# A two-block network on one core: later heads' keys, values and queries made between the blocks of the first attention, keys scaled head by head, other chunks for the first and the last product

## The reference

```python
# block 1, layer 0: s=1 FFN, s=2 pooling + latent attention, s=3 FFN
# block 1, layer 1: s=4 FFN, s=5 gated convolution, s=6 FFN
# block 2:          s=7 FFN, s=8 Fourier mixing + grouped attention, s=9 FFN, final norm
x = x + 0.5 * (silu(h @ w_gate) * (h @ w_up)) @ w_down      # h = rms_norm(x), width 2816 or 2752
# s=2
u, q_lat, kv_lat, k_rope = split(rms_norm(x) @ w_in)        # 512, 384, 256, 32 columns
q  = rms_norm(q_lat)  @ w_q_up                              # 8 heads of 96
kv = rms_norm(kv_lat) @ w_kv_up                             # 8 heads of 64 (key) + 64 (value)
q, k = norm by head, then rotate the last 32 of the 96 columns
attn = softmax(q @ k.T * 96**-0.5, causal) @ v
x = x + concat(pool_out, attn) @ w_out
```

## Time and profile before

| what | us |
|---|---|
| median of 3 runs | 2751.69 |
| the profiled execution's own time | 2747.63 |
| its span, first to last instruction | 2745.8 |
| PE busy | 2713.2 |
| DVE busy | 1341.3 |
| ACT busy | 900.1 |
| POOL busy | 134.3 |
| weights and inputs read, MB | 248.16 |

### The profile page before, as it was taken

One profiled execution on the slowest core, in us unless ns is written; L12 is line 12 of the kernel. 1 busy time (PEld: TensorE's weight loads), 2 busy tenths in 40 slices (PEclk: granted clock), 3 DMA queues, 4 the chain that ended last, 5 costly groups with the idle time before them and its releaser, 6 DMA issues.

```text
span 2745.8 us, 31449 instructions
## 1 busy us (share of the span) xinstructions
PE 2713.2 (99%) x12604; PEld 2258.1 (82%) x12604; DVE 1341.3 (49%) x1917; ACT 900.1 (33%) x1286; POOL 134.3 (5%) x133
## 2 busy tenths in 40 slices
PE   8999999999999999999999999999999999999998
PEld 7888878888888888888888888888878888888787
DVE  5444358764443444434555444344443378644433
ACT  4232226542222323222223323232222247423221
POOL 0000004400000000000000000000000035000000
PEclk9999999999999999999999999999999999999999
DMA  4333232023333333323332233333332321233322
GB/s 153 100 97 96 91 92 76 24 92 101 99 96 97 98 99 95 100 89 103 92 100 92 92 99 97 98 90 104 98 91 90 98 71 44 74 101 95 92 86 72
DMA packets 283105, 252.30 MB, mean 92 GB/s; under 512 B 8272, under 2 KB 280784, under 8 KB 282960
## 3 DMA queue, kind: packets, MB, share of 16 engines
q1 hardware_dynamic: 282960, 250.29, 29.8%
HBM read 248.16 MB, written 2.10 MB: 91 GB/s over the span
## 4 chain that ended last, share of the span: by engine, by line
PE 95%; DVE 2%; ACT 1%; issue 1%; DMA 0%; POOLq 0%; POOL 0%; DVEq 0%; SPq 0%; ACTq 0%
PE bank L415 31%; PE bank L417 31%; PE bank L416 31%; PE bank L545 1%; ACT wh L884 0%; DVE X L1269 0%; DVE wl L1260 0%; PE bank L457 0%; PE bank L603 0%; PE bank L604 0%; ACT Xh L912 0%; DVE a_KT L1272 0%; DVE acc L1269 0%; ACT Xh L915 0%; DVE Xl L1269 0%
## 5 line engine op out<-in xcount | busy, mean ns | idle before, releaser
L1260 DVE TENSOR_TENSOR wl<-raw,wh 128x1024 fp32r<-128x1024 f32 (+4 forms) x491 | 572.4, 1180 | 926.7 <-ACT wh L884 926.2
L415 PE MATMUL bank<-Xh,wl 128*128 128x512 f32 (+1 forms) x2544 | 994.4, 391 | 11.6 <-DVE wl L1260 6.6
L417 PE MATMUL bank<-Xh,wh 128*128 128x512 f32 (+1 forms) x2544 | 991.7, 390 | 0.0
L416 PE MATMUL bank<-Xl,wh 128*128 128x512 f32 (+1 forms) x2544 | 991.4, 390 | 0.0
L884 ACT ACTIVATE wh<-raw 128x1024 fp32r<-128x1024 f32 (+4 forms) x491 | 491.5, 1016 | 961.5 <-PE bank L417 947.9
L415 PEld LDWEIGHTS bank<-Xh,wl 128*128 128x128 f32 (+1 forms) x2544 | 476.1, 187 | 116.1 <-issue 8.8
L417 PEld LDWEIGHTS bank<-Xh,wh 128*128 128x128 f32 (+1 forms) x2544 | 475.9, 187 | 102.9
L416 PEld LDWEIGHTS bank<-Xl,wh 128*128 128x128 f32 (+1 forms) x2544 | 476.1, 187 | 101.0
L415 PE MATMUL bank<-Hh,wl 128*128 128x512 f32 (+3 forms) x1078 | 415.9, 386 | 3.4 <-DVE wl L1260 3.4
L416 PE MATMUL bank<-Hl,wh 128*128 128x512 f32 (+3 forms) x1078 | 415.5, 385 | 0.0
L417 PE MATMUL bank<-Hh,wh 128*128 128x512 f32 (+3 forms) x1078 | 415.4, 385 | 0.0
(11 more groups left out here) (289 smaller groups left out, 1563.2 us busy)
## 6 DMA issues: line engine op xcount, KB each, us to landing
raw<-in_ffn_w_up SPq DMA_DIRECT2D x128, 512.0 KB, 3.8
raw<-in_ffn_w_gate SPq DMA_DIRECT2D x127, 512.0 KB, 3.6
raw<-in_ffn_w_down SPq DMA_DIRECT2D x114, 512.0 KB, 3.5
raw<-in_c_w_in SPq DMA_DIRECT2D x24, 512.0 KB, 3.6
raw<-in_w_in SPq DMA_DIRECT2D x10, 512.0 KB, 4.1
raw<-in_ffn_w_down SPq DMA_DIRECT2D x16, 256.0 KB, 2.7
raw<-in_a_w_in SPq DMA_DIRECT2D x8, 512.0 KB, 3.7
raw<-in_a_w_out SPq DMA_DIRECT2D x8, 512.0 KB, 3.3
```

What stands on the lines that cost most here:

```text
L415: e.matmul(o, ll, rh, start=start, stop=False)
L416: e.matmul(o, lh, rl, start=False, stop=False)
L417: i = e.matmul(o, lh, rh, start=False, stop=stop)
L1260: e.tensor_tensor(lo, src, hi.bitcast(F), ALU.subtract).then_inc(wlo.up(("w", n)), 1)
```

## The change

1. **Start.** The first `w_gate` chunks hold 1, 1, 2 and 4 row blocks, so there is one chunk more, and x and chunks are issued in another order. The counts of `use` follow.
2. **Keys and values.** Only heads 0 to 3 are made before the attention. Heads 4 to 7 (`keys_values(1)`) move into `later`, between the queries of heads 3 to 5 and of heads 6 and 7. `fill` takes one step for each block in place of two half steps, so it runs from block 0 to block 11.
3. **Scaling by head.** `finish_keys(h)` scales one head for all four token tiles: head 0 within `queries(0)`, heads 1 to 3 after the first three query tiles of `queries(1)`, heads 4 to 7 within `queries(2)`.
4. **Order on PE.** `first_half(1)` moves behind the first two transposes; `first_half` 2 to 7 run 4 turns later. The ring begins in another order. The high part of the turned weights gets a buffer of its own (`aPTh`), and the latents move in `aRB`.
5. **`mixer_out`**, for s=2 and s=8: squares of tiles 4 and 5 come later, low parts of tiles 4 and 5 earlier, and the last `use` lies between.
6. **End.** `last_tile` takes each of its chunks when it gets to it.

```diff
+FIRST = ((0, 128), (128, 256), (256, 512), (512, 1024))
-            got += chunks(wg, 0, 128, 0, 256, 1) + chunks(wg, 128, 512, 0, 256, 3) + chunks(wg, 512, D, 0, 256, 4)
+            got += [c for k0, k1 in FIRST for c in chunks(wg, k0, k1, 0, 256, 4)]
...
             def early_at(self, k, when):
-                t = (k - when) // 4 + self.early
-                return t if (k - when) % 4 == 0 and self.early <= t < KT else None
+                k -= when + (4 if self.causal else 0)
+                t = k // 4 + self.early
+                return t if k % 4 == 0 and self.early <= t < KT else None
...
             def last_tile(s, hi, lo, kt, tail):
-                stay = [chunk() for _ in range(3)]
-                rows = [(h, l, kk) for _, h, l, nk in stay for kk in range(nk)]
+                rows = []
...
-                    for k, (h, l, kk) in enumerate(rows):
+                    for k in range(kt):
+                        if k == len(rows):
+                            _, h, l, nk = chunk()
+                            rows += [(h, l, kk) for kk in range(nk)]
+                        h, l, kk = rows[k]
...
             def attention(m, prepare, fill):        # PE
-                    next(fill, None)
+                    if not m.causal:
+                        next(fill, None)
                 for k in range(4):
                     prepare(k)
+                if m.causal:
+                    first_half(s, 1)
                 for k in range(m.ahead):
                     prepare(k + 4)
                     start(k)
-                for _ in fill:
-                    pass
...
             def mixer_mla(s):                       # PE
+                n, h, l, _ = chunk()
+                for t in range(4):
+                    token_major(4 + t, ("kv", s, 0, t), latents(3, 2, t), h, l, 512, n if t == 3 else None)
+                squares_summed(3, ("stat", s, "q"), aacc[0], ("lsq", s, 2))
-                ring[0] = BankRing((6, 4, 5, 7, 0, 1, 2, 3))
+                ring[0] = BankRing((0, 1, 2, 4, 5, 6, 7, 3))
+                def keys_values(c):
+                    n, h, l, _ = chunk()
+                    for t in range(4):
+                        name = ("kv", s, c, t)
+                        token_major(ring[0].take(name), name, latents(3, 2, t), h, l, 512, n if t == 3 else None)
+                        yield
+                        ring[0].free(name)
                 def later():
                     yield from queries(1)
+                    yield from keys_values(1)
                     yield from queries(2)
...
                     else:                           # in prepare: a head's keys
-                        w.wait_ge(dve, ("keys", s, h // 4, 3))
-                        w.wait_ge(pool, ("keys", s, h // 4, 3))
+                        w.wait_ge(dve, ("keys", s, h))
+                        w.wait_ge(pool, ("keys", s, h))
...
                 def queries(g):                     # DVE, one token tile
                         reduce_square(assq[:, t, hs], nh * 96, 96)
                         rotate(q4[:, :, 64:96], ...)
+                        if g == 0 and t == 0:
+                            finish_keys(0)
...
+                        if g == 1 and t < 3:
+                            finish_keys(1 + t)
+                        if g == 2:
+                            finish_keys(4 + t)
...
+                for t in range(KT):                 # DVE, mixer_out
+                    if t % 2 == 0 and t < 6:
+                        use()
+                    add_to_x(s, t, banks[bank_of["down", s, t]], ("down", s, t), ("x", s, t))
+                    if 1 <= t <= 4:
+                        x_low(s, t - 1, gain, "half", s, 7)
+                        x_square(s, t - 1)
+                    elif t >= 6:
+                        x_low(s, t - 2, gain, "down", s, 7)
+                use()
+                for t in (6, 7):
+                    x_low(s, t, gain, "down", s, 7)
                 for t in range(4, KT):
-                    x_low(s, t, gain, "down", s, 7)
-                for t in range(6, KT):
                     x_square(s, t)
...
             load_x(0)                               # SP
             fetch(0)
+            fetch(1)
             load_x(1)
-            fetch(1)
-            for t in (2, 3):
+            fetch(2)
+            for t in (2, 3, 4):
                 load_x(t)
-            fetch(2)
-            for t in range(4, KT):
+            fetch(3)
+            for t in range(5, KT):
                 load_x(t)
+            fetch(4)
```

More of the change, by code:

```diff
@@ L708, in latents @@
                         w.wait_ge(dve, ("lat", s, k))
[L709 to L716, removed]
-                ring[0] = BankRing((6, 4, 5, 7, 0, 1, 2, 3))
+                    return [tuple(aRB[:, i, sl] for i in latent_at(k)) for k in range(k0, k0 + kt)]
+                n, h, l, _ = chunk()
[3 more added lines that the diff above has]
+                ring[0] = BankRing((0, 1, 2, 4, 5, 6, 7, 3))
                 def queries(g):
@@ L755, in prepare @@
                     ring[0].free(name)
+                for _ in queries(0):
+                    pass
+                first_half(s, 0)
                 attention(mA, prepare, later())
@@ L981, in turned_high @@
                     w.wait_ge(mm, ("turn", s, k))
-                    w.wait_ge(mm, ("out", s, k // 4 - 1, k % 4 // 2) if k >= 4 else ("ahead", s))
+                    if k >= 4 or not m.causal:
+                        w.wait_ge(mm, ("out", s, k // 4 - 1, k % 4 // 2) if k >= 4 else ("ahead", s))
                     copy(turned(m, k)[0], banks[bank_of["turn", s, k]][:, 0:m.cols(k)].rearrange("p (c q) -> p c q", q=128),
@@ L1047, in latent @@
                     w.wait_ge(dve, ("z", s, n))
-                    copy(aRB[:, n, :], z[:, :], ("lat", s, n), scale=g)
+                    copy(aRB[:, latent_at(n)[0], :], z[:, :], ("lat", s, n), scale=g)
                     square(z[:, :], aacc[n // 3][:, :] if n % 3 == 0 else None)
@@ L1077, in mixer_mla, with keys_values @@
                     copy(Xh[:, g, :], banks[g][:, :], ("ch", s, g), scale=col("pscale", g))
-                for c in range(2):
+                def keys_values(c):
                     use()
@@ L1090, in mixer_mla @@
                              scale=r1)
+                        yield
+                for _ in keys_values(0):
+                    pass
                 def queries(g):
@@ L1566, in mixer_mla, with finish_keys, keys_values @@
                         ("cl", s, g), ("read", ("pool", s, g)))
-                def finish_keys(c, t):
-                    hs = slice(4 * c, 4 * c + 4)
-                    w.wait_ge(act, ("knope", s, c, t))
-                    w.wait_ge(pool, ("rk", s, c))
-                    tt(aktm[:, t, hs, 0:64], aktm[:, t, hs, 0:64], bc(ark[:, t, hs], 2, [128, 4, 64]), ALU.mult,
-                       ("keys", s, c, t))
-                for c in range(2):
+                def finish_keys(h):
+                    hs = slice(4 * (h // 4), 4 * (h // 4) + 4)
+                    w.wait_ge(act, ("knope", s, h // 4, 3))
+                    w.wait_ge(pool, ("rk", s, h // 4))
+                    tt(aktm[:, :, h, 0:64], aktm[:, :, h, 0:64], bc(ark[:, :, h], 2, [128, 4, 64]), ALU.mult, ("keys", s, h))
+                def keys_values(c):
                     use()
@@ L1578, in mixer_mla @@
                     for t in range(4):
-                        v4 = banks[(4 * c + t + 4) % 8][:, :].rearrange("p (h c) -> p h c", h=4)
+                        bank = banks[4 + t if c == 0 else bank_of["kv", s, c, t]]
+                        v4 = bank[:, :].rearrange("p (h c) -> p h c", h=4)
                         reduce_square(assk[:, t, hs], 256, 64)
@@ L1621, in later @@
                     yield from queries(1)
-                    for t in range(4):
-                        finish_keys(1, t)
+                    yield from keys_values(1)
                     yield from queries(2)
```

117 lines of the change are left out of this document (49 added, 68 removed).

## The result

The changed kernel takes 2756.98 us (median of 14 runs, 2753.81 to 2759.57), the kernel before 2748.89 us (14 runs, 2745.85 to 2752.33): ratio 1.0028, 95% interval 1.002 to 1.0037. It is 8.1 us slower, where 0.2 us less was forecast. Its profiled execution took 2757.28 us, 9.7 more than that of before, with a span of 2755.5 us.

What follows compares the result with a forecast made beforehand. PE bounds the kernel, busy 2713.2 of 2745.8 us, so only idle time and lower-clock matmuls can be won. End -5.0, hand-overs -3.2, start -0.9, attention +8.9 give -0.2: 2751.4 us, range 2742 to 2758 for 8 of 10.

Steps and rivals of the forecast that it cites:

- End, -5.0: Last tile: 3.4 us of PE idle time go, and 1.5 us more without the clock drop; at least -3.4.
- Hand-overs, -3.2: Into s=3 and s=9: PE's 1.6 us loss waiting for x's low part goes twice; between -2.6 and -3.3.
- Start, -0.9: Program start: a smaller second weight chunk no longer ends an idle time of 1.07 us; between 0 and -1.3.
- if the clock rises at the same instant: Start: with the clock rising when it did, slow matmuls fill the idle time, 0.7 us won; after the same work, 1.26.
- Attention up to the first transpose: First attention: PE idle 3.0 us for the last query tile, copy wait of 1.28 covered; 1.5 us lost.
- Blocks 0 to 3: First attention: PE waits 2.5 us for head 1's keys, then 2.9 us for their bank at the third query tile.
- Blocks 4 to 11: Rest of first attention: 1.6 us copy wait, two late banks; score 12 is 6.9 late, whole attention loses 8.9 us.
- two waits of 2.2: First attention, turn 2: PE asks for two banks that DVE empties late, each about 2.2 us.
- a wait that would be covered: First attention, before 532.20: a later `first_half` covers a wait of 0.75 us.
- the bound of 12: First attention: loss of 12 us if waits make the clock fall once or twice.
- rival 3: Attention, 446 to 466: three waits make the clock fall and stay down, +7, 2758.4 us; chance 0.12.
- Rivals 1 and 2: Attention: waits only move, attention 0, 2742.5 us, chance 0.17; moved work fills 5 us of idle time, 2737.5 us, chance 0.10.

Runs made afterwards that it cites:

- e11_rest_again: e1_rest profiled a second time, unchanged: 2739.29 us (profiled execution).
- e2_filler: The changed kernel with matmuls of no use ahead of the five longest PE waits of the attention: 2752.07 us, ratio 1.0012 to the kernel before.
- e6_bank: e3_key1 with the third later query tile taking the bank of score 0 instead of that of head 1's keys: 2750.27 us, ratio 1.0002.
- e10_head_powers: The changed kernel with the POOL powers for the key factors made head by head, 128x4 in place of 128x16: 2754.31 us, ratio 1.0020.
- e9_all_filler: e7_all with 20 matmuls of no use ahead of four of its remaining waits: 2743.37 us, ratio 0.9985.
- e7_all: The changed kernel with head 1's keys scaled earlier, those of heads 4 to 7 later, and head 0's orders on PE, DVE and POOL mended: 2747.71 us.
- e1_rest: The kernel before with all of the change but its attention (start, both hand-overs, end): 2739.53 us, ratio 0.9970.
- e4_factors: The changed kernel with the keys of heads 4 to 7 scaled two steps later on DVE: 2754.94 us, ratio 1.0023.
- e3_key1: The changed kernel with head 1's keys scaled at the end of the first query group, heads 2 and 3 one step earlier: 2753.11 us, ratio 1.0019.
- e12_after_again: The changed kernel profiled a second time, unchanged: 2755.04 us (profiled execution).

## Why the prediction was wrong

The forecast difference was -0.2 us, the measured one +8.1, +9.7 in the profiled execution. That the time itself, 2756.98 us, lies only 5.6 us from the 2751.4 forecast is luck: the base moved by 2.8 us the other way (the median of before was 2751.69 in three runs, 2748.89 in 14).

- **End, -5.0: right** (-5.1, here and in 11 of the 12 other traces with this end), both terms of it, the idle time and the clock at 1.00.
- **Hand-overs, -3.2: right in size.** There is no wait for x any more. Into s=3 it gives 1.7 us (137.99 to 136.26). Into s=9, from the sum of s=8 to the next, before took 183.2 us; the 13 traces with the new hand-over took 181.4 to 181.5 in six and 182.9 to 183.1 in seven. In the seven, after among them, the clock fell in s=8 behind waits of about 1.3 and 0.8 us that all of them have (0.57 in 2283 to 2287 of after). So 1.8 are won and 1.6 lost again in about half of the executions; what decides it is not shown.
- **Start, -0.9: too small,** -2.4. The step "if the clock rises at the same instant" was wrong: it rose 3.9 us earlier. That the missing idle time did it is not shown: in the 13 traces that have this start the clock rises between 8.8 and 13.3 us, and late in some without any idle time there (12.5 in e11_rest_again). The first sum comes between 24.1 and 26.4 us, so against the one trace of before the gain is 0.7 to 3.0.
- **Attention up to the first transpose: right.** 2.77 us idle for 3.0, DVE idle 2.05 us before the scaling of head 0, the copy wait of 1.28 covered.
- **Blocks 0 to 3: right.** 2.63 for 2.5, 2.66 for 2.9, with the releasers that were named.
- **Blocks 4 to 11: the step that failed.** The forecast is best held against e2_filler, where the clock stays up. Scores 8 and 12 in before (its sum at 437.68):

```profile
475.27 0.31 PE L415 MATMUL bank<-a_KT,a_QT 96*128 96x128 f32 x1
...
483.42 0.30 PE L415 MATMUL bank<-a_KT,a_QT 96*128 96x128 f32 x1
```

and in e2_filler (its sum at 435.59):

```profile
475.08 0.31 PE L424 MATMUL bank<-a_KT,a_QT 96*128 96x128 f32 x1
...
492.57 0.31 PE L424 MATMUL bank<-a_KT,a_QT 96*128 96x128 f32 x1
```

Counted from the sums, score 8 is 1.9 us late and score 12 is 11.2, where 6.9 was forecast. The work put off behind each counts as well: 36 matmuls of 192 columns at score 8 (4.1 us), 12 of 512 columns at score 12 (the 2.7 us of the forecast). So 6.0 us were lost up to score 8, and the forecast's own terms say the same: 1.5, 2.5, 2.9 less the 0.49 of before, 1.6 less 1.96. From score 8 to 12, 8.0 us were lost, where the forecast had only two waits of 2.2, in all 4.4. In after, the waits there are 3.33 before turn 2 and 1.88 before score 10, the two it named, and 0.54 before the transposes of keys and 0.89 before a query tile (1.87 with the clock up), which it didn't name. The second power, behind which DVE stood 2.23 us, took 3.75 us for the 3.0 it reckoned with. So the waits of this part were priced 3.6 us too low.

- **A slip in the sum.** The forecast's own terms give 10.4 us lost up to score 12; it wrote 6.9 + 2.7 = 9.6. That is 0.8. Behind score 12 it took off 0.75 for a wait that would be covered; 0.2 came, so 0.5 more.
- **The clock** was given no place in the sum, only in the bound of 12 and as rival 3, with a chance of 0.12. It cost 5.4 us. Rival 3 came nearest (2758.4): its condition, a granted clock below 0.8 between 446 and 466, was met with 0.78. It erred in that the clock "stays down": it came back each time, and fell once more in 487 to 495, outside the place.
- 8.9 + 3.6 + 0.8 + 0.5 + 5.4 = 19.2 of the 19.1 us measured (155.40 - 136.26).
- **Rivals 1 and 2** (waits only move, it works as a filler) fell. Single waits do move in part (e6_bank, e10_head_powers), but not as a whole. And the moved work won nothing as a filler even with the orders mended: e9_all_filler still loses 6.6 us.

The rule of the Trainium skill (TensorE: Matmul & The Clock Gate, "Part 1: The HAM clock gate") weighed in the prediction, that activity has to hold the clock up, agrees with e2_filler and e9_all_filler, where useless matmuls brought the time at the lower level from 17.1 us (after) and 20.5 us (e7_all) to 0 and 3.4. The prediction gave it little weight on the evidence of one execution in which 1.96 us of idle time left the clock at 1.00; e1_rest shows the same wait with the other outcome.

## What to carry to other kernels

When PE waits about 2 us or more in a stretch that is otherwise full, or several times 0.5 to 1.6 us in short order (e4_factors, s=8), price the wait at its length and, behind it, some microseconds at half rate in about every second execution, as here; a single trace in which the clock held is no evidence that it always will. Matmuls of no use into a bank that is free, laid into the wait, are a cheap cure for the clock alone (5.4 us in the changed kernel's profiled execution, 3.7 in its median); they don't shorten the wait. And when a schedule by hand is checked at one point, count the work that has been put off behind that point as lost too.

## What was new about the hardware

- The fall of the clock behind idle time differs between executions of one program: behind 1.96 us it fell in e1_rest, not in e11_rest_again nor in before; behind 2.77 to 2.83 us ahead of the first transposes in three kernels (after, e4_factors, e6_bank) and not in e3_key1 and e12_after_again; in s=8, behind 1.3 and 0.8 us, in 7 of all 14 traces, for 1.6 us each time.
- What the lower level costs in this attention can be read off ten traces: 0.45 us for each us at it, from 0 to 27.3 us, apart from the waits.
- The power on POOL has a cost that its size doesn't explain. Of 128x16 it took 3.72 and 3.75 us in after, 3.96 and 3.01 in before. Of 128x4 (e10_head_powers), a quarter of that, it took 1.83 us at first and three in a row took 2.97, 0.99 each. The profile's spans on POOL are rough:

```profile
440.95 1.83 POOL L1916 TENSOR_TENSOR a_rk<-a_vk,half 128x4 f32<-128x4 f32 x1 [6.95 <-DVE a_small L1299]
...
448.58 2.97 POOL L1916 TENSOR_TENSOR a_rk<-a_vk,half 128x4 f32<-128x4 f32 x3
```
